# Moving the low parts of one stage's weights from Pool to VectorE, in a hybrid decoder step

## The reference

```
u = rmsnorm(x);  q, k, v, qi, ki, wi, z, xbc, dt = split(u @ w_in)      # 2048 x ~6800
att = sparse attention: the indexer scores (qi, wi, ki) pick 128 keys for each token,
      softmax(q.k * scale + rel_bias, others masked) @ v                 # 8 heads of 128
y   = Mamba-2 scan over xbc and dt                                       # 16 heads of 64
h   = x + concat(att, rmsnorm(y * silu(z))) @ w_out
out = h + (silu(f @ w_gate) * (f @ w_up)) @ w_down,  f = rmsnorm(h)
```

## Time and profile before

| | |
|---|---|
| median of 3 runs | 2904.67 us (2886.48 to 2906.92) |
| the profiled execution | 2905.41 us, span 2903.6 us |
| mean granted clock of TensorE | 0.973 |
| TensorE busy | 2748.0 us, 95% |
| VectorE busy | 1787.6 us, 62% |
| ScalarE busy | 1027.1 us, 35% |
| Pool busy | 391.8 us, 13% |

### The profile page before, as it was taken

How to read it: one execution, slowest core, us unless ns; L and a number is a source line. 1 busy time by engine, 2 the same in 40 slices (tenths; PEclk the granted TensorE clock), 3 DMA queues, 4 the chain that set the end, 5 groups by cost and what they waited for, 6 DMA issues and landing times.

```text
span 2903.6 us, 49432 instructions
## 1 busy us (share of the span) xinstructions
PE 2748.0 (95%) x20329; PEld 2641.8 (91%) x20329; DVE 1787.6 (62%) x2616; ACT 1027.1 (35%) x1517; POOL 391.8 (13%) x166
## 2 busy tenths in 40 slices
PE   8999999999998977998999999999999999999997
PEld 7977898888888867998999999999999989999997
DVE  3322599455555545247777777777777787776423
ACT  5233221333333323224443443434434443443222
POOL 2322233211111101341000000000000000000231
PEclk9999999999999988999999999999999999999999
DMA  6322231655555546432334334333333464644521
GB/s 230 106 74 76 75 107 52 183 157 159 161 156 156 157 119 212 132 128 84 112 120 141 112 112 130 123 121 112 124 122 104 146 201 144 236 150 154 200 104 66
DMA packets 394449, 388.83 MB, mean 134 GB/s; under 512 B 25405, under 2 KB 354725, under 8 KB 391160
## 3 DMA queue, kind: packets, MB, share of 16 engines
q1 hardware_dynamic: 375432, 364.20, 39.8%
q10 hardware_dynamic: 18800, 21.58, 2.1%
HBM read 319.11 MB, written 68.00 MB: 133 GB/s over the span
## 4 chain that ended last, share of the span: by engine, by line
issue 66%; PE 16%; POOL 7%; SPq 4%; DMA 3%; DVE 3%; ACT 0%; ACTq 0%; POOLq 0%; DVEq 0%
PE PS L918 6%; PE PS L1350 5%; POOL WL L807 4%; POOL WL L832 2%; SPq L545 2%; SPq L541 1%; DMA ssm_sample<-h 1%; DMA kca<-in_cache_k 1%; DVE mt L2182 1%; PE PS L1103 1%; DVE ex L2174 1%; DMA mixS<-xs 1%; PE PS L1311 1%; DVE h L2289 1%; PE PS L1143 1%
## 5 line engine op out<-in xcount | busy, mean ns | idle before, releaser
L1366 PE MATMUL PS<-xo_t,WH 128*128 128x288 f32 x2544 | 517.0, 298 | 14.1 <-DVE WL L2338 3.7
L918 PE MATMUL PS<-AH,WH 128*128 128x288 f32 (+1 forms) x2208 | 496.2, 307 | 17.3 <-POOL WL L807 4.9
L918 PE MATMUL PS<-AH,WL 128*128 128x288 f32 (+1 forms) x2208 | 479.1, 299 | 0.0
L918 PE MATMUL PS<-AL,WH 128*128 128x288 f32 (+1 forms) x2208 | 479.1, 299 | 0.0
L1366 PEld LDWEIGHTS PS<-xo_t,WH 128*128 128x128 f32 x2544 | 412.3, 190 | 15.8 <-issue 15.8
L918 PEld LDWEIGHTS PS<-AH,WH 128*128 128x128 f32 (+1 forms) x2208 | 361.2, 192 | 39.4 <-issue 29.3
L1366 PE MATMUL PS<-xo_x,WH 128*128 128x288 f32 x1936 | 389.2, 295 | 2.6 <-DVE xo_x L2426 1.0
L1366 PE MATMUL PS<-xo_t,WL 128*128 128x288 f32 x1272 | 377.5, 297 | 0.0
L918 PEld LDWEIGHTS PS<-AL,WH 128*128 128x128 f32 (+1 forms) x2208 | 361.7, 192 | 0.0
L918 PEld LDWEIGHTS PS<-AH,WL 128*128 128x128 f32 (+1 forms) x2208 | 361.5, 192 | 0.0
L2338 DVE TENSOR_TENSOR WL<-WRAW,WH 128x1024 fp32r<-128x1024 f32 x201 | 245.8, 1223 | 109.2 <-ACT WH L1766 108.0
(11 more groups left out here) (371 smaller groups left out, 3723.9 us busy)
## 6 DMA issues: line engine op xcount, KB each, us to landing
WRAW<-in_w_gate SPq DMA_DIRECT2D x22, 2048.0 KB
WRAW<-in_w_up SPq DMA_DIRECT2D x22, 2048.0 KB
WRAW<-in_w_down SPq DMA_DIRECT2D x32, 1024.0 KB
WRAW<-in_w_in SPq DMA_DIRECT2D x14, 2048.0 KB, 8.3
raw<-in_w_in SPq DMA_DIRECT2D x48, 512.0 KB, 4.4
kca<-in_cache_k SPq DMA_DIRECT2D x256, 64.0 KB, 1.9
vca<-in_cache_v SPq DMA_DIRECT2D x256, 64.0 KB, 2.5
WRAW<-in_w_out SPq DMA_DIRECT2D x16, 1024.0 KB, 10.4
```

The source lines that it names most:

```text
L918: last = nc.tensor.matmul(G[gslot][0:width, h, 0:HALF], wt[:, half if slot is None else slot, k % 8, 0:width], act[:, k, h * HALF:(h + 1) ...
L1366: last = mm(out, wt[:, k, :], act[:, m, k, :], start=(j in (0, 1, 3) and k == 0 and wt is wh and m == 0), stop=(k == 7 and wt is wl), skip ...
```

## The change

Pool makes the first seven low parts of the stage: the six of head 0 and n = 0 of head 1. The other 41 are made by VectorE: a new function `low3(i, n)` makes the low part n of head i, and is called at six fixed places of `turn_dve`. Pool then waits until all low parts of the stage are there before it goes on with the third stage. ScalarE's, TensorE's and SP's orders stay as they were.

```diff
@@ Pool
-            with pool.Fori(0, 8) as i:
-                for n in range(6):
-                    lower8(pool, 6 * i + 58 + n, raw3[:, n % 3, :, :], n % 2)
-
+            for n in range(7):
+                lower8(pool, 58 + n, raw3[:, n % 3, :, :], n % 2)
+
+            pool.wait_ge(s["w_lo"], C3)
@@ VectorE
+            def low3(i, n):
+
+                c = 6 * i + 58 + n
+                dve.wait_ge(s["w_hi"], c + 1)
+                dve.wait_ge(s["w_lo"], c)
+                tt(WL[:, n % 2, :, :], raw3[:, n % 3, :, :], WH[:, n % 2, :, :].bitcast(F32), ALU.subtract).then_inc(s["w_lo"], 1)
+
@@ turn_dve
                 logits(i, 2)
                 logits(i, 3)
+                if units:
+                    low3(i, 1)
                 twait(dve, "lnew", i)
...
                 seg(i, 0)
                 seg(i, 1)
                 if units:
+                    low3(i, 2)
                     take(i, 0, qT)
...
                 for n in range(4):
                     weigh(i, n)
                     seg(i, n + 2)
+                if units:
+                    low3(i, 3)
 
                 twait(dve, "su", i)
...
                 ttaken(cp(els[:, :], els[:, :]), "su")
+                if units:
+                    low3(i, 4)
                 for c in range(3):
...
                     if c == 0 and units:
                         take(i, 1, kT)
+                        low3(i, 5)
...
                 if units:
+                    if i < 7:
+                        low3(i + 1, 0)
                     take(i, 2, vT)
```

## The result

The changed kernel takes 2908.84 us (median of 20 runs, 2902.89 to 2919.37) against 2897.09 us (20 runs, 2886.48 to 2908.55) for the kernel before: a ratio of 1.004, 95% interval 1.0026 to 1.0053, so 11.6 us more (7.5 to 15.4). The forecast was 2913 us, and 7.7 us more. Medians and ratios here are of fast runs: three executions of the kernel before beside e9 to e12, of 3338 to 4415 us at a granted clock of 0.55 to 0.75, are left out.

A forecast was written before the change was run, and what follows sets the result against it. A turn was bounded by the last one's end, SP's queue, the keys, then TensorE's second half. Terms -4.3 + 7.5 + 3.0 + 1.5 = +7.7 us on the profiled 2905.4 gave 2913 us, range 2890 to 2935.

The forecast's parts named there:

- Term 1: Second half of turns: VectorE's `ex` and `mt` stalls beside Pool go, and TensorE's waits for `xs`; gain 4.3 us.
- first rival: VectorE's `ex` and `mt` stalls were worth their whole length: 29 us saved, 2876 us, or 2887 with terms 2 and 3; 6%.
- Term 2: VectorE's closing run: the next head's low part delays the state updates TensorE awaits, 1.25 us in six turns; cost 7.5 us.
- Term 4: Turn's end: more TensorE idle time lowers the clock, so the fifth turn goes like the others; cost 1.5 us (0 to 4.5).
- Term 3: SP's queue: low part n = 3 holds a raw load and the cached-key loads behind it, up to 0.9 us; cost 3.0 us.
- All low parts hidden: Turn's end hidden too, because the decode result comes earlier and TensorE has other work: 2901 us; 15%.
- The clock lasting into the next product: Turn's end wait lowers TensorE's clock into the next head's product, 6 us in six turns: 2949 us; 7%.
- a low part that waits on VectorE for a cast: VectorE becomes the order's bound, softmax held 1.25 us in the second halves too: 5 to 9 us more, 2920 us; 8%.

The follow-up runs named there:

- e9: e3 with the third value block's three matmul pairs made twice ahead of `fin`; 2885.68 us, ratio 0.9964 to the kernel before.
- e12: e9 with the eight `su` matmuls made three times in turns 2 to 6; 2881.91 us, ratio 0.9951 to the kernel before.
- e3: Changed kernel with the next head's low part n = 0 behind the state updates and n = 3 ahead of the decay tiles; 2892.82 us, ratio 0.9990 to before.
- e6: e3 with two low parts of a turn, n = 5 and the next head's n = 0, back on Pool; 2898.84 us, ratio 0.9999 to before.
- e4: Changed kernel with two unused VectorE maxima ahead of the next head's low part n = 0, turns 1 to 6; ratio 1.0093 to the kernel before.
- e1: Changed kernel with only the next head's low part n = 0 moved behind the state updates; 2900.14 us, ratio 1.0012 to the kernel before.
- e11: Changed kernel with the second value block's two matmul pairs made twice, in the sixth product, meant as control; 2905.69 us, ratio 1.0026 to before.
- e10: Kernel before with the third value block's three matmul pairs made twice ahead of `fin`; ratio 0.9993 to the kernel before.
- e5: Changed kernel with two unused VectorE maxima ahead of low part n = 3, turns 1 to 7; 2915.82 us, ratio 1.0060 to the kernel before.
- e2: Changed kernel with only low part n = 3 moved ahead of the decay tiles; 2900.86 us, ratio 1.0020 to the kernel before.
- e8: Changed kernel with the third value block's three matmul pairs made twice ahead of `fin`; 2897.39 us, ratio 1.0000 to the kernel before.

## Why the prediction was right, and where it was off

**What bounds the kernel** was right: the end of the turn, SP's queue and the keys, TensorE's second half. That Pool's low parts were not waited for was right too. That 2913 and the measured 2908.84 lie 4 us apart is in part luck: the forecast started from the profiled execution, 8.3 us above the median of 20 runs, and put the change 3.9 us too low, and the two errors have opposite signs.

**Term 1, the stalls** (forecast -4.3 us): the stalls and both waits went. e3, in which only this is left, reads -2.9 us (-7 to +1.5), and e6, with eight of the thirteen stalls of this term back, +2.6. The size fits but is not shown to differ from zero. e3 excludes the first rival, 4.2 us a turn.

**Term 2, the closing run** (+7.5): shown by e4, in which all of the added time reaches TensorE. The direct part was 1.02 us a turn and not 1.25 (1.36 - 0.34), 6.1 us in six turns: start to start the low part takes 1.14 us, and `vT` to the update 0.66 where it took 0.79.

**Term 4, the clock** (+1.5) is the term that was mis-sized. Terms 2 and 4 were forecast at 9.0 together and measured at 8.1 by e1, which looks like a hit. But filling half of the wait, which leaves the update as late as it was, gives back 11.6 us (7 to 16), and a third of it, in e11, 4.1 (-1 to 9). A part of these gains the kernel before would have had as well, so they are not the price of the change. I had taken the turn ends of one trace as typical, six low and one high, and let only the one fall. e10 speaks against that: with filling there is little to gain in the kernel before. In the changed kernel's trace all six ends behind the 1.36 us wait are low, and each costs 1.4 to 1.5 us (one 2.5) against the 5.7 of an end at the upper clock. If 19 of 40 are low behind the short wait, as in all traces together, the change pushes down some three of the six, an estimate of 6 x 21/40 x 1.5 = 4.7 us where the term had 1.5. The direct wait and the clock cannot be added up from these runs, since a shorter end seems in part given back in the wait for the keys (213.9 us before, 216.2 in e1).

**Term 3, SP's queue** (+3.0): the mechanism holds in turn 1, where the key loads are issued 0.9 us later, as forecast, but the transposes come 1.5 later. TensorE's wait for these keys grew from 0.32 to 1.86 us in turn 1, but fell from 3.11 to 2.34 in turn 2. In turns 2 to 6 the load is held by 0.2 to 1.5 us (forecast 0.1 to 0.9), but e5 shows that 2.25 us more in each turn hardly move the keys there. The step that failed is the one from "issued later" to "lands later". e2 nonetheless measures 5.9 us (1 to 11), and e5 5.8 where the first turn explains 1.5; where the rest lies stays open.

**The rivals.** All low parts hidden: excluded by e1 and e4. The clock lasting into the next product: in the changed kernel's trace it did not; in turn 3 the lower level was over by 751 us, and the next logits start at 753.45. But it can happen: in the trace of e2, with the same 1.35 us wait, two of the ends took 9.35 us, and the first five pairs of the next product were slow too: 0.83 us, then 0.65 to 0.68, where the changed kernel's trace has 0.50 to 0.52, then 0.42 to 0.43. The last, a low part that waits on VectorE for a cast, did not happen: the 41 low parts have 0.3 us of idle time before them in all.

## What to carry to other kernels

Moving work to an engine that is half idle costs nothing only where that engine's next result is not awaited; look for its runs without a gap, and put the work behind them. A wait on TensorE costs more than its length when it takes the clock down for the work behind it: if it cannot be removed, fill it with harmless matmuls, and prove it with a control that has the same matmuls elsewhere, after looking in its trace that the wait is as long as without them; here it was not. Where a kernel's runs spread by 0.8%, the turn ends or clock levels of one trace are a sample, not a price.

## What was not expected of the hardware

- Six useless matmul instructions per turn, 0.66 us more of work, were worth 11.6 us (7 to 16) in seven turns. After a wait of 0.68 us and one of 0.89, TensorE's granted clock stays at 1.00 (e8, six of six). After 1.36 and 0.89 it is 0.59 to 0.76 in the mean, from `fin` to the logits, in all six such ends of the changed kernel (7.0 to 8.2 us); after 0.91 and 0.89 four of six are low (e11). After 0.34 and 0.89 both occur in the same trace. So the length of the wait alone does not decide: 0.68 us behind the doubled block was always up, 0.34 without it was not.
- A VectorE operation that starts 0.18 us after a Pool operation of 2.4 us is held to its end (2.30 for 0.29 us); two that started within 0.4 us before it are not (0.59 us), and one that started 0.08 us after it took 2.40 us (e6).
- A load held in SP's queue for 2 to 4 us more than before (e5, turns 2 to 6) hardly made the loads behind it land later; in the one such stretch looked at, in the kernel before, the DMA engines' share was 1.13.
